# The second chunk's attention beside the expert gathers of a two-block network: new order of its phases, and a new table of the gathers they stand at

## What is computed

```python
proj = h @ w_in[l]                                   # queries, keys, values of two branches a and b
oa = global_attention(rope(rms_norm(qa)), rope(rms_norm(ka)), va)   # branch 0 in the kernel
ob = window_sink_attention(qb, kb, vb, sink[l], slopes)             # branch 1 in the kernel
mix = concat([rms_norm(oa), rms_norm(ob)]) @ w_o[l]
h = layer_norm(ALPHA * h + mix)
# peer_ffn, for each chunk of 128 tokens
q = (x @ wq).reshape(128, 8, 2, 128)
sc = einsum('chpd,hpnd->chpn', q, sub_keys)          # then top 16 of 128 twice, top 16 of 256
u_sel, v_sel = u[eidx], v[eidx]                      # 8 * 16 = 128 experts for each token
w = softmax(top_s) * gelu(einsum('chkd,cd->chk', u_sel, x))
ffn = einsum('chk,chkd->cd', w, v_sel)
h = layer_norm(ALPHA * h + ffn)
```

## Time and profile before

| | |
|---|---|
| three runs, us | 3029.99, 3025.13, 3027.5 (median 3027.5) |
| the profiled execution's own time | 3026.93 us |
| its span, first to last instruction | 3025.1 us |
| granted TensorE clock over the span | 0.822 of 2.4 GHz |
| busy in the span | PE 2137.6 us, DVE 1585.9, ACT 835.9, POOL 858.3 |
| layer 0, gathers 0 to 255 by `dots` | 190 to 996 us |
| layer 1, gathers 0 to 255 by `dots` | 1150 to 1925 us |
| DMA over the span | 907.20 MB, 300 GB/s |

### The profile page before, as it was taken

How to read it: one execution, slowest core, us unless ns; L and a number is a source line. 1 busy time by engine, 2 the same in 40 slices (tenths; PEclk the granted TensorE clock), 3 DMA queues, 4 the chain that set the end, 5 groups by cost and what they waited for, 6 DMA issues and landing times.

```text
span 3025.1 us, 33379 instructions
## 1 busy us (share of the span) xinstructions
PE 2137.6 (71%) x11604; PEld 1066.5 (35%) x11604; DVE 1585.9 (52%) x3294; ACT 835.9 (28%) x2338; POOL 858.3 (28%) x739
## 2 busy tenths in 40 slices
PE   6865686866676673586776776698897776666674
PEld 3532242222111361233332332368783532222221
DVE  5246657667564446755989876456544421121111
ACT  2213333333333313333343443323210111111110
POOL 1112344333353002333553554111020112122221
PEclk9867787977786786788798898798998798788887
DMA  7476699998999416699899899711113299999994
GB/s 273 187 301 265 269 422 421 400 421 325 419 419 421 192 56 264 254 414 407 324 382 353 355 403 421 291 59 58 54 57 127 113 408 397 390 388 381 377 383 147
DMA packets 133026, 907.20 MB, mean 300 GB/s; under 512 B 23664, under 2 KB 24176, under 8 KB 32112
## 3 DMA queue, kind: packets, MB, share of 16 engines
q0 software_dynamic: 86976, 553.74, 46.1%
q1 hardware_dynamic: 45872, 351.24, 28.8%
HBM read 895.95 MB, written 40.37 MB: 310 GB/s over the span
## 4 chain that ended last, share of the span: by engine, by line
PE 37%; DMA 27%; DVE 24%; ACT 6%; issue 3%; POOL 1%; SPq 1%; DVEq 0%; ACTq 0%; POOLq 0%
PE ps L155 35%; DMA ring<-in_peer_uv,idx_u 11%; DMA ring<-in_w_gu 7%; DVE ring L1483 6%; DVE arena L76 4%; ACT arena L125 4%; DMA ring<-in_w_down 3%; DVE arena L1483 2%; DMA ring<-in_w_mod 2%; DMA arena<-in_peer_uv,idx_u 2%; PE ps L158 2%; DVE iu L113 1%; DVE arena L109 1%; DVE arena L97 1%; DMA arena<-in_w_gu 1%
## 5 line engine op out<-in xcount | busy, mean ns | idle before, releaser
L155 PE MATMUL ps<-ring,arena 64*64 64x512 f32 (+3 forms) x4576 | 927.8, 774 | 500.4 <-ACT arena L125 346.3
L155 PE MATMUL ps<-arena 128*128 128x128 f32 (+8 forms) x3208 | 569.9, 507 | 192.2 <-ACT arena L125 127.9
L2644 POOL DMA_INDIRECT ring<-in_peer_uv,idx_u x384 | 436.6, 1137 | 604.8 <-PE ps L155 559.7
L1483 DVE CUSTOM_DVE_ANT_0 ring<-ring,h 128x1024 f32<-128x1024 f32 x384 | 479.7, 1249 | 244.6 <-DMA ring<-in_peer_uv,idx_u 194.6
L155 PEld LDWEIGHTS ps<-ring,arena 64*64 64x64 f32 (+3 forms) x4576 | 226.5, 157 | 1019.3 <-ACT arena L125 623.0
L125 ACT ACTIVATE arena<-arena 128x1 f32<-128x1 f32 (+3 forms) x1053 | 272.9, 259 | 856.7 <-DVE arena L1483 740.4
L155 PEld LDWEIGHTS ps<-arena 128*128 128x128 f32 (+4 forms) x3208 | 289.7, 180 | 443.0 <-ACT arena L125 244.4
L125 ACT ACTIVATE arena<-ps 128x512 f32<-128x512 f32 (+3 forms) x192 | 104.8, 546 | 821.1 <-PE ps L155 749.8
L76 DVE TENSOR_TENSOR arena<-arena,ps 128x512 f32<-128x512 f32 (+1 forms) x154 | 91.0, 591 | 445.4 <-ACT arena L125 360.7
L155 PE MATMUL ps<-ring,hT 128*128 128x512 f32 (+2 forms) x832 | 284.9, 501 | 3.8 <-ACT hT L125 2.4
L2644 POOL DMA_INDIRECT arena<-in_peer_uv,idx_u x128 | 148.0, 1156 | 312.0 <-PE ps L155 169.9
(11 more groups left out here) (129 smaller groups left out, 1579.4 us busy)
## 6 DMA issues: line engine op xcount, KB each, us to landing
ring<-in_w_gu SPq DMA_DIRECT2D x98, 1024.0 KB, 30.3
ring<-in_w_down SPq DMA_DIRECT2D x52, 1024.0 KB, 23.6
ring<-in_peer_wq SPq DMA_DIRECT2D x16, 2048.0 KB, 11.1
arena<-in_w_gu SPq DMA_DIRECT2D x30, 1024.0 KB, 27.9
ring<-in_w_mod SPq DMA_DIRECT2D x24, 1024.0 KB, 6.9
ring<-in_w_in SPq DMA_DIRECT2D x10, 2048.0 KB, 16.1
arena<-in_w_in SPq DMA_DIRECT2D x6, 2048.0 KB, 11.4
ring<-in_w_o SPq DMA_DIRECT2D x6, 2048.0 KB, 10.1
```

The lines of the kernel that those rows point to most:

```text
L155: return self.e.matmul(o, lhsT, rhs, start=start, stop=stop, skip_group_check=True)
L1483: v.done(v.e.tensor_tensor_reduce(out=row, in0=row, in1=h[:, n // 128, :], scale=1.0, scalar=0.0, op0=ALU.mult, op1=ALU.add, accum_out=aa[ ...
L2644: g.e.indirect_dma_start(out=landing(l, n), out_offset=None, in_=d["peer_uv"], in_offset=bass.IndirectOffsetOnAxis(ap=idx_u[:, n:n + 1], a ...
```

## The change

`SECOND_AT`, `CONTEXT_AT`, `NEXT_AT` and `STATES_AT` replace the rule in `beside`: `second_chunk` now has 29 phases, one at each odd gather from 3 to 59; in layer 0 the context's phases stand at every third gather from 62 to 221 (54, filled up by `padded`) and those of `next_rows` at every third from 222 to 249 (10); in layer 1 the 76 phases of `context_states` stand at the gathers from 62 to 251 whose last digit is 2, 4, 7 or 9.

Inside a phase DVE's part comes first, then ACT's, then PE's, and what PE makes in one phase is taken by DVE or ACT in the next. The two branches of the attention overlap: `scores` of branch 0 stands between `spread` and `spread_back` of branch 1, and the half of `out_rows` that needs only branch 1 stands beside `values` and `spread` of branch 0. `queries` takes two of its four parts in each phase in place of one. `spread_at` puts branch 1 of chunk 1 elsewhere (20480), and the phases of `second_chunk` may take the banks 2 to 7 (`MORE`). `rope` on POOL gets a yield.

```diff
-def beside(l, n):
-
-    if n < 72:
-        return 1 if n >= 2 and n % 3 else 0
-    if l:
-        return 1 if n < 250 and n % 2 == 0 else 0
-    return 1 if n in range(72, LAST_ROWS, 3) or n in range(LAST_ROWS, 252, 2) else 0
+SECOND_AT, CONTEXT_AT, NEXT_AT = range(3, 61, 2), range(62, 222, 3), range(222, 252, 3)
+STATES_AT = [n for n in range(62, 252) if n % 5 in (2, 4)]
+def beside(l, n):
+    return 1 if n in SECOND_AT or n in ((*CONTEXT_AT, *NEXT_AT), STATES_AT)[l] else 0
...
         def spread_at(br, c):
-            o = 7872 if c else 11968 if br else 12992
+            o = (20480 if br else 7872) if c else 11968 if br else 12992
...
             def second_chunk(l):
 
-                yield
-                for br in (1, 0):
-                    scores(l, br, 1, OTHERS)
-                    yield from idle(3)
-                    turned_powers(l, br, 1, OTHERS)
-                    yield from idle(2)
-                    values(l, br, 1, OTHERS)
-                    yield
-                    spread(l, br, 1, OTHERS)
-                    yield
-                    spread_back(l, br, 1, OTHERS)
-                    yield from idle(2)
-                yield from out_rows(l, 1, OTHERS)
-                yield from idle(5)
-                turned_rows(2 * l + 1, 1, OTHERS)
+                scores(l, 1, 1, MORE)
+                yield
+                yield
+                turned_powers(l, 1, 1, MORE)
+                yield
+                values(l, 1, 1, MORE)
+                yield
+                spread(l, 1, 1, MORE)
+                yield
+                scores(l, 0, 1, MORE)
+                yield
+                spread_back(l, 1, 1, MORE)
+                yield
+                turned_powers(l, 0, 1, MORE)
+                yield
+                rows = out_rows(l, 1, MORE)
+                next(rows)
+                values(l, 0, 1, MORE)
+                yield
+                next(rows)
+                spread(l, 0, 1, MORE)
+                yield
+                yield
+                spread_back(l, 0, 1, MORE)
+                yield
+                next(rows)
+                yield
+                next(rows)
+                yield from idle(4)
+                turned_rows(2 * l + 1, 1, MORE)
                 yield
                 for hf in range(2):
                     for i in (2 * hf, 2 * hf + 1):
-                        yield from queries(l, i, 1, OTHERS)
+                        q = queries(l, i, 1, MORE)
+                        next(q)
+                        next(q)
                         yield
-                    key_scores(l, 1, hf, OTHERS)
-                    yield
+                        for _ in q:
+                            pass
+                        yield
+                    key_scores(l, 1, hf, MORE)
+                    yield
+                yield
...
                 biases(1)
                 yield
-                for br in (1, 0):
-                    maxima(l, br, 1)
-                    yield from idle(2)
-                    scaled(l, br, 1)
-                    yield from idle(2)
-                    turned_powers(l, br, 1)
-                    yield from idle(2)
-                    mean_squares(l, br, 1)
-                    yield
-                    mix_factors(l, br, 1)
-                    yield
-                    mixed(l, br, 1)
-                    yield
-                yield from idle(4)
+                maxima(l, 1, 1)
+                yield
+                scaled(l, 1, 1)
+                yield
+                turned_powers(l, 1, 1)
+                yield
+                yield
+                mean_squares(l, 1, 1)
+                yield
+                mix_factors(l, 1, 1)
+                maxima(l, 0, 1)
+                yield
+                mixed(l, 1, 1)
+                scaled(l, 0, 1)
+                yield
+                turned_powers(l, 0, 1)
+                yield
+                yield
+                mean_squares(l, 0, 1)
+                yield
+                mix_factors(l, 0, 1)
+                yield
+                mixed(l, 0, 1)
+                yield
+                yield
                 add_rows(l, 1)
```

More of the change, by code:

```diff
@@ L193 @@
 GATHERS = 8
-SUMS, OTHERS = ((0, 1), (2, 3)), (4, 5, 6, 7)
+SUMS, OTHERS, MORE = ((0, 1), (2, 3)), (4, 5, 6, 7), (2, 3, 4, 5, 6, 7)
 X_AT, Y_AT = ((4, 8), (12, 16)), ((12, 16), (4, 8))
@@ L223, in idle, with padded @@
         yield
+def padded(n, *gens):
+    for _ in chain(*gens):
+        n -= 1
+        yield
+    assert n >= 0
+    yield from idle(n)
 class Side:
@@ L747, in next_rows @@
                 turned_keys(l, 1, 0, OTHERS)
+                turned_keys(l, 0, 0, OTHERS)
+                yield
                 turned_queries(l, 1, 0, OTHERS)
-                yield from idle(3)
-                turned_keys(l, 0, 0, OTHERS)
                 turned_queries(l, 0, 0, OTHERS)
+                yield
                 yield
@@ L1384, in second_chunk @@
                 yield
-                for br in (1, 0):
-                    maxima(l, br, 1)
-                    yield from idle(2)
-                    scaled(l, br, 1)
-                    yield from idle(2)
-                    turned_powers(l, br, 1)
-                    yield from idle(2)
-                    mean_squares(l, br, 1)
-                    yield
-                    mix_factors(l, br, 1)
-                    yield
-                    mixed(l, br, 1)
-                    yield
-                yield from idle(4)
-                add_rows(l, 1)
-                yield from norm_of(2 * l + 1, 1)
+                maxima(l, 1, 1)
[22 more added lines that the diff above has]
+                yield
+                yield
+                add_rows(l, 1)
+                norm = norm_of(2 * l + 1, 1)
+                next(norm)
+                yield
+                next(norm)
+                yield
+                next(norm)
+                yield
+                for _ in norm:
+                    pass
                 v.tell(("used", "ln1", l))
-                yield from idle(2 + 18)
+                yield from idle(12)
             def next_rows(l):
+                yield
+                v.wait_ge(*at("features stored"))
                 take_kt(hT, ("hT", 2 * l), 0, 0)
-                v.wait_ge(*at("features stored"))
                 yield
@@ L1409, in next_rows @@
                 take_rows(l, 0, 0)
+                k = rope(l, "k", 0)
+                next(k)
                 yield
-                yield from rope(l, "k", 0)
+                for _ in k:
+                    pass
                 yield
-                yield from rope(l, "q", 0)
+                q = rope(l, "q", 0)
+                next(q)
+                yield
+                for _ in q:
+                    pass
+                yield
+                yield
                 yield
                 biases(0)
-                yield from idle(4)
+                yield
             def topk(groups, n, vals, ids, src, alt):
@@ L2267, in next_rows @@
                 take_keys(l, 1, 0)
+                take_keys(l, 0, 0)
+                yield
                 take_queries(l, 1, 0)
-                yield from idle(3)
-                take_keys(l, 0, 0)
                 take_queries(l, 0, 0)
@@ L2605, in first_chunk @@
                 if l == 0:
-                    rope(0, "k", 0)
-                rope(l, "k", 1)
+                    run(rope(0, "k", 0))
+                run(rope(l, "k", 1))
                 if l == 0:
-                    rope(0, "q", 0)
+                    run(rope(0, "q", 0))
                 for br in (1, 0):
                     mix_rsqrt(l, br, 0)
-                rope(l, "q", 1)
+                run(rope(l, "q", 1))
                 rsqrt(st["rs"][:, 0:1], ("var", 2 * l + 1, 0), "rstd", 2 * l + 1, 0)
             def second_chunk(l):
-                yield
-                for br in (1, 0):
-                    yield from idle(6)
-                    mix_rsqrt(l, br, 1)
-                    yield from idle(3)
+                yield from idle(5)
+                mix_rsqrt(l, 1, 1)
+                yield from idle(5)
+                mix_rsqrt(l, 0, 1)
                 yield from idle(6)
                 rsqrt(st["rs"][:, 1:2], ("var", 2 * l + 1, 1), "rstd", 2 * l + 1, 1)
-                yield from idle(3 + 1 + 18)
+                yield from idle(13)
             def next_rows(l):
+                yield from idle(3)
+                yield from rope(l, "k", 0)
+                yield
+                yield from rope(l, "q", 0)
                 yield from idle(4)
-                rope(l, "k", 0)
-                yield
-                yield
-                rope(l, "q", 0)
-                yield from idle(5)
             def peer(l, background):
```

59 lines of the change are left out of this document (35 added, 24 removed).

## The result

The changed kernel takes 2941.6 us (median of four runs, 2941.3 to 2942.0), the kernel before 3028.6 beside it (3025.1 to 3030.0). The ratio is 0.9715, with a 95% interval of 0.9698 to 0.9731. So it is faster by 87 us by the medians, or 85 us between the two profiled executions (3026.9 and 2941.5 us), where 68 were forecast. The time lies in the stated range.

A forecast was written before the change was run, and what follows sets the result against it. Before gather 32 DVE's waits for PE hold the gathers; at layer 1's gathers 80 to 175 DVE's own work binds. Gains 22 + 20 + 8 + 14 + 4 = 68 us from 3026.9 gave 2959 us, range 2925 to 2985.

The forecast's parts named there:

- Products one phase later: First gathers of both layers: DVE takes PE's products one phase later, most waits close; gain 22 us layer 1, 20 layer 0.
- The step that took 10.9 us of wait at `add_rows` as worthless: Layer 1, gather 37: DMA engines carried 410 of 423 GB/s, so removing this wait gives back only 1.6 us.
- The kept waits: Layer 1, branch 0: `mean_squares` still waits about 4 us and `add_rows` another 1, 5 us off the gain.
- The first rival: First stretches: waits move and don't close, giving 12 and not 42 us, total 2989 us; chance 0.20.
- `queries` at twice the work: Gathers 37 to 59: PE's 63 us of work fits narrowly under 65 us of transfers; cost 0.
- The sign I named: PE's granted clock at gathers 37 to 59 is 0.9 or more if right, under 0.8 at `queries` if wrong.
- `ctx_tab`: Layer 1, scan's start: table load gets four more gathers, 6 to 7 us of 16.65 us wait stay; gain 8 us.
- The scan thinned: Layer 1, gathers 80 to 175: 38.4 phases for 48, at 2.15 us each, rest moved past 175; gain 14 us.
- a third of these gathers already ran at the pace of the DMA: Layer 1, gathers 80 to 175, citing 96 to 111: cut the thinning's gain from 20.6 to 14 us.
- The context's work in layer 0: Moved ten gathers earlier, two phases come before routing starts at 130; gain 4 us, ends -4 and 11.
- Two signs: Layer 1: first 64 gathers take 205 to 212 us; wait for `ctx_tab` is 5 to 8 us at gather 62.
- The sign of the other rule: GpSimd shares SBUF interfaces with VectorE: denser stretch slows 128 `dots` by 0.025 us, 3 us; not taken into the sum.

The follow-up runs named there:

- e1: Changed kernel with the new `second_chunk`, but context, `next_rows` and scan phases at the gathers of the kernel before: 2966.7 us, 0.9795 of the kernel before.
- e4: Changed kernel, but DVE takes `mean_squares` of both branches in the phase in which PE makes `spread`: 2953.1 us, 0.9751 of the kernel before.
- e5: Changed kernel with every second quarter of `queries` of chunk 1 made twice, 8 quarters more for PE in each layer: 2944.3 us, 0.9712 of the kernel before.
- e9: Changed kernel with layer 1's scan begun at gather 67, not 62, at the same two gathers of five: 2942.1 us, 0.9716 of the kernel before.
- the repeat: The changed kernel measured again, unaltered, beside other runs on a second chip: 2940.1 us, 0.9712 of the kernel before.

## Why the prediction came out as it did

The time lies in the range, and the largest term is right in its mechanism; the sizes are less good than the columns by time suggest, because the `wq` blocks changed columns (above).

**Products one phase later: right in its mechanism, too small in size.** 22 and 20 us were put for layers 1 and 0. By time gathers 0 to 47 gained 21.2 and 23.3, which looks exact; but they carried some 3 and 2.3 MB more, and in uncovered time the gain is 28.3 and 28.7, 57 where 42 stood. e1, with this part alone at the old tables, measured 60 us with some 5 of `ctx_tab` in it. The step that took 10.9 us of wait at `add_rows` as worthless, since the DMA engines were full at gather 37, held: uncovered time at gathers 32 to 47 was 1.6 us and is 0. The gain lies before gather 32, 26.7 us in layer 1, where 23.3 us of waits for PE closed; the forecast had 25.4 there and took 5 off again. The kept waits, 4 and 1 us, came as 2.1 and 1.6. The remaining 3 us aren't traced. e4 shows the mechanism by its reverse: the hand-over at `mean_squares` put back costs 11 us over both layers. The first rival, that waits only move, is dead; waits for PE fell to a tenth.

**`queries` at twice the work: right at 0.** I gave the transfers as the cover, with 2 us of room. e5 put 16 us more on PE in each layer, and the median rose by 2.6 us, within the intervals, with the first signs of a cost in its slowest execution. The sign I named, a granted clock of 0.9 or more, was wrong: it was 0.82, and that meant room, not danger.

**`ctx_tab`: 6.1 for 8 in uncovered time, and for another reason.** By time the column gained 13.5 us, but 7 of them are transfers that now pass before gather 48. I priced the wait by how much shorter it would get. It got shorter by 6.4 us, which agrees with 6.1 only by chance: in the kernel before the transfers ran at full pace while it lasted, and what cost time was DVE's work behind it. e9, which puts gathers' waits in the place of what is left, gains nothing.

**The scan thinned: 18.7 for 14, and 15.3 in the repeat.** The price of a phase, 2.15 us, is 2.0 by the runs. The step that is doubtful is "a third of these gathers already ran at the pace of the DMA". The window named, gathers 96 to 111, did gain less than its share: 1.9 us, where two phases less would give 4. But gathers 80 to 95 gained 7.9 for two phases, so the stretch as a whole lost nothing by it. DVE's waits had none for DMA there: DVE and transfers took about equally long. That what DVE saves is used in a neighbouring window, as up to eight gathers may be ahead, fits and is not shown.

**The context's work in layer 0: 3.7 for 4, by luck.** The columns after gather 48 changed by -4.9, +13.0 and -11.8 us, mostly because work and transfers crossed their bounds. In uncovered time they hold 24.6 us before and 26.3 with the change, no gain. The place that I had named, gathers 144 to 159, takes 48.9 us where it took 47.9. Against e1 with the old table, 30.4 us, it is 4 better; with one execution of each the sign is open. DVE's waits at the two convolutions are 8.8 and 5.9 us where they were 3.5 and 9.6.

**Outside both stretches: 4.4 us** that I had at 0, and that are the spread of an execution (above).

In uncovered time the 85 us between the two executions are, rounding apart, 28.3 + 28.7 for the products, 6.1 at gathers 48 to 79 of layer 1, 17.0 for the scan and 2.8 past it, -1.7 for layer 0 after gather 48, and 4.4 outside. Of the surplus of 17 over the forecast, 15 come from the products, 6 from the scan and behind it and 4.4 from the rest of the program, against 2 and 6 us too much at `ctx_tab` and the context. So 2959 was near in part because terms that were too small and too large made up for one another.

Two signs failed beside the clock: the first 64 gathers of layer 1 take 214 us and not 205 to 212, as the wait for `ctx_tab`, which stood past gather 71, now lies among them, and that wait is 10.2 us and not 5 to 8.

By the Trainium skill ("TensorE: Matmul & The Clock Gate", section "Why this matters for your kernels") closing the waits should shorten the products too. It did, as `spread` shows with 0.95 us for 1.87, and the granted clock of the first 64 gathers, 0.80 for 0.76; 0.9 of the 1.9 us by which the kept wait came shorter are this. The sign of the other rule, on GpSimd beside VectorE, hardly shows where it was expected: `dots` at gathers 0 to 47 takes 1228 ns where it took 1225. It shows, in both kernels, where the scan's products on GpSimd stand, as the 1316 and 1289 ns of gathers 80 to 175 tell.

## What to carry over

Where engines in order work through one list of phases, let the engine at the end of the chain hand its product to the next phase; each hand-over inside a phase costs the whole way round, here 3 to 9 us. The length of a wait is not its price: ask whether the transfers are full while it lasts and whether the waiting engine is short of time after it. An engine that hardly waits in a stretch is bound by its sum of work there, so work moved out of it gained its duration here, as it went to a place where that engine does wait. And before two columns of time are compared, look at what the transfers carried in each: here a load that moved made two terms of the sum look exact that were not.

## What was not expected of the hardware

TensorE's busy time under a partial load doesn't tell how much more it could do. With 339 matmul records in 58 us it was busy 49.0 us at a granted clock of 0.82; with 429 in 57 us, 54.5 us at 0.92. Sixteen more records in a phase take 1.78 us in a dense stretch (5.62 us for 48 and 3.84 for 32, by PE's timelines), so these 90 are some 10 us of work, and they cost it 5.5 us of busy time and the kernel's median nothing that can be measured.

A `dots` that meets a product on GpSimd can take up to twice its time and more. Of the 208 `dots` of layer 1 from gather 48 on, 196 take 1.2 to 1.4 us in the kernel before and 12 take 1.9 to 2.8; each of the 12 overlaps one of GpSimd's 128x512 products, and in the changed kernel it is the same, 12 of 208. One of those of the kernel before and the product beside it:

```profile
1464.33 2.78 DVE L1483 CUSTOM_DVE_ANT_0 ring<-ring,h 128x1024 f32<-128x1024 f32 x1
...
1464.74 1.28 POOL L134 TENSOR_TENSOR arena<-arena,cst 128x512 f32<-128x512 f32 x1
```

Seven others in the kernel before overlap such a product too and take no longer than usual.
